# Two directions of a chunked recurrence in one level: a changed issue order on TensorE, and a side product made chunk by chunk

## The reference

```
def wkv_scan(state, r, w, a, b, k, v, reverse):
    def step(S, inp):
        r_t, w_t, a_t, b_t, k_t, v_t = inp
        sa = jnp.einsum('bhvk,bhk->bhv', S, a_t)
        S = S * w_t[:, :, None, :] + sa[..., None] * b_t[:, :, None, :] + v_t[..., None] * k_t[:, :, None, :]
        return S, jnp.einsum('bhvk,bhk->bhv', S, r_t)
    xs = tuple(jnp.moveaxis(t, 1, 0) for t in (r, w, a, b, k, v))
    state, y = lax.scan(step, state, xs, reverse=reverse)
```

```
    bonus = jnp.einsum('bthn,btdhn,hn->bth', rh, kh, r_k)[..., None] * v.reshape(B, T, RWKV_HEADS, RWKV_HEAD)
```

## Time and profile before

| | us |
|---|---|
| timed runs | 2593.86, 2598.66, 2600.04 (median 2598.66) |
| the profiled execution's own time | 2595.06 |
| its span | 2593.3 |
| PE busy | 2276.3 (88%) |
| DVE busy | 1158.6 (45%) |
| ACT busy | 727.4 (28%) |
| POOL busy | 390.9 (15%) |

### The profile page before, as it was taken

How to read it: one execution, slowest core, us unless ns; L and a number is a source line. 1 busy time by engine, 2 the same in 40 slices (tenths; PEclk the granted TensorE clock), 3 DMA queues, 4 the chain that set the end, 5 groups by cost and what they waited for, 6 DMA issues and landing times. The chain is left out here.

```text
span 2593.3 us, 47213 instructions
## 1 busy us (share of the span) xinstructions
PE 2276.3 (88%) x19058; PEld 1503.0 (58%) x19058; DVE 1158.6 (45%) x2561; ACT 727.4 (28%) x1698; POOL 390.9 (15%) x441
## 2 busy tenths in 40 slices
PE   6999989889979998899898679999888988888885
PEld 3444455548844444466565568877658876554453
DVE  3877765575542113632211563244576532531113
ACT  2010155465531002032222120024455531222220
POOL 0000000044340001122221000000034320222210
PEclk8999999999989999999999889999989999898997
DMA  9455401210016103699998642312310043899994
GB/s 379 195 213 237 166 33 43 81 43 5 4 50 259 73 0 118 253 385 397 371 355 316 271 173 98 129 67 94 103 39 5 4 157 125 348 414 384 380 376 170
DMA packets 80360, 474.27 MB, mean 183 GB/s; under 512 B 17296, under 2 KB 29200, under 8 KB 51728
## 3 DMA queue, kind: packets, MB, share of 16 engines
q1 hardware_dynamic: 55280, 419.82, 41.2%
q0 software_dynamic: 24864, 51.43, 5.2%
HBM read 439.99 MB, written 61.08 MB: 193 GB/s over the span
## 5 line engine op out<-in xcount | busy, mean ns | idle before, releaser
L2851 PE MATMUL xp_psG<-moe_ring,rt_xt 128*64 128x256 f32 (+1 forms) x2048 | 328.9, 406 | 39.7 <-DMA moe_ring<-in_moe 38.9
L2851 PEld LDWEIGHTS xp_psG<-moe_ring,rt_xt 128*64 128x64 f32 (+1 forms) x2048 | 228.5, 163 | 118.1 <-issue 56.8
L599 PE MATMUL win_ps<-h,win_ring 128*128 128x512 f32 x512 | 226.2, 600 | 5.4 <-PEq L292 5.4
L659 DVE SCALAR_TENSOR_TENSOR mod_acc<-ada_ring,cv_silu,mod_acc 128x512 f32<-128x512 f32 x280 | 198.0, 748 | 10.9 <-issue 0.4
L3108 DVE TENSOR_TENSOR rt_sg<-rt_sg,xp_psG 128x128 f32<-128x128 f32 x84 | 24.2, 288 | 335.9 <-ACT rt_sg L2925 335.9
L599 PEld LDWEIGHTS win_ps<-h,win_ring 128*128 128x128 f32 x512 | 97.0, 192 | 125.6 <-issue 125.6
L2872 PE MATMUL xp_psY<-moe_ring,rt_aT 128*64 128x512 f32 (+1 forms) x512 | 162.1, 602 | 2.9 <-DVE rt_aT L3115 2.9
L1274 POOL MEMSET ml_w<- 128x1536 f32 x4 | 5.4, 1376 | 765.3 <-POOLq L973 765.3
L2919 ACT ACTIVATE rt_xt<-xp_psT 128x512 f32<-128x512 f32 x168 | 90.9, 595 | 95.2 <-PE xp_psT L2836 89.4
L2178 PE MATMUL sc_ps<-sc_NT,sc_XI 64*64 64x64 f32 x2560 | 110.4, 225 | 8.2 <-issue 5.7
L2505 DVE TENSOR_TENSOR mg_gateb<-mg_gateb,mg_psY 128x512 f32<-128x512 f32 (+1 forms) x48 | 26.6, 554 | 192.1 <-PE mg_psY L2462 186.8
(11 more groups left out here) (539 smaller groups left out, 4302.0 us busy)
## 6 DMA issues: line engine op xcount, KB each, us to landing
moe_ring<-in_moe SPq DMA_DIRECT2D x128, 1536.0 KB, 16.1
ada_ring<-in_ada SPq DMA_DIRECT2D x22, 2048.0 KB, 14.8
win_ring<-in_win SPq DMA_DIRECT2D x20, 2048.0 KB, 8.2
cb_yg<-y_rows SPq DMA_DIRECT2D x16, 1024.0 KB, 13.1
mg_ring<-in_mg SPq DMA_DIRECT2D x16, 768.0 KB, 4.5
mg_wo<-in_wo SPq DMA_DIRECT2D x2, 4096.0 KB, 14.4
pr<-y_rows SPq DMA_DIRECT2D x8, 1024.0 KB, 17.7
ml_gate_ring<-in_mg SPq DMA_DIRECT2D x12, 512.0 KB, 3.6
```

Of the source, the lines that this page charges most:

```text
L599: last = pe.matmul(ps[:, n % NB, first(n):T], ring[:, j % 2, c, m * P:(m + 1) * P], h[:, c, first(n):T], start=c == 0, stop=c == KD - 1)
L659: last = dve.scalar_tensor_tensor(out=acc[:, a % 2, s], in0=aring[:, a % 3, c], scalar=weight, in1=acc[:, a % 2, s], op0=ALU.mult, op1=ALU ...
L2851: last = pe.matmul(psG[at:at + m, u % 2, 0:2 * P].rearrange("p (q n) -> p q n", q=2), xt[:, u % 2, c, at:at + m], ring[:, slot, c:2 * KD:K ...
```

## The change

1. The levels of both directions are issued together: `level(n, m)` waits for both directions, then issues d = 0 straight and d = 1 crossing, by turns. `place` lets direction 1 cross at every level, 0 and 5 too. The `across` waits are gone.
2. What `between` does is now put behind a level, for both directions: state products at m = 1, value products at m = 2, the transposes at m = 3, nothing at m = 4. The semaphore `onto` parts straight from crossing products in psR. The transposes are now products of 64x64 with the identity, in all four quarters; `first` parts the two groups of them.
3. ACT makes the right side at m = 2 between its two copies, and two strided copies of bk at m = 4 after each copy.
4. `state_and_rows` is split: state product and rows of the chunk before level 0, rows of the state behind it. `update` is split: `add_products` waits for the state product only, `decay` waits for the rows of the state.
5. `hat` has two buffers.
6. POOL makes the bonus per chunk of 64 tokens, all channels, between the operands of the steps; `queries` tells when a chunk's inputs are free.

The core of the diff:

```diff
-        hat = sb("hat", [P, KC, 2, L])
+        hat = [sb(f"hat{b}", [P, KC, 2, L]) for b in range(2)]
...
                 def step(n):
                     for m in range(1, 5):
                         for d in range(2):
                             copied(d, n, m)
-                            if n == 0 and m == d + 1:
+                            if n == 0 and m == 1:
                                 exponentials(d, 1)
-                            if m == 3:
-                                token_major(0, n, d)
+                            if m == 2:
+                                right_side(d, n)
                             if m == 4:
-                                token_major(*((0, n, 2), (1, n, 0))[d])
...
+                def bonus(j):
+
+                    f = j // NCH * NCH + max(j % NCH, NCH - 1 - j % NCH)
                     for d in range(2):
-                        operands(pool, d, n)
...
+                        w(pool, d, "queries", f)
+                    col = slice(j * L, (j + 1) * L)
+                    both, key = aa[:, 0, :, col], pr[:, K_T:K_T + KC, col]
...
+                ready = {3: (1,), 4: (2,), 5: (0,), 6: (3, 5), 7: (6, 4, 7)}
+                for n in range(1, NST):
+                    for d in range(2):
+                        operands(pool, d, n)
+                    for j in ready.get(n, ()):
+                        if j in outs:
+                            bonus(j)
...
-                def update(d, n):
-                    w(dve, d, "sy", n)
+                def add_products(d, n):
+
+                    w(dve, d, "s", n)
                     dve.tensor_tensor(S2[d][:], S[d][:], psS[d], ALU.add)
-                    dve.drain()
+
+                def decay(d, n):
+
+                    if n in outs:
+                        w(dve, d, "rows", n)
...
+                    def place(d, r, m):
+
+                        return HD - r if d and m % 2 else r
...
+                    for hp in range(KC):
+                        if m < 5:
+                            for d in range(2):
+                                for r in (0, HD):
+                                    to, wt, x = operands_of(d, hp, r)
+                                    pe.matmul(psW[d][to:to + HD, hp], wt, x, start=True, stop=True)
+                        for d in range(2):
+                            for r in (0, HD):
+                                to, wt, x = operands_of(d, hp, r)
+                                last = pe.matmul(psWT[d][to:to + HD, hp], x, wt, start=True, stop=True)
+                            if hp == KC - 1:
+                                last.then_inc(sem[d]["nn"].sem, 1)
...
                 def step(n):
                     for m in range(1, 6):
+                        level(n, m)
                         for d in range(2):
-                            level(d, n, m)
+                            between(d, n, m)
                     for d in range(2):
                         if n + 1 < NST:
                             matrices(d, n + 1)
                         corrections(d, n)
                     for d in range(2):
-                        state_and_rows(d, n)
-                        if n + 1 < NST:
-                            level(d, n + 1, 0)
+                        state_product(d, n)
+                        rows_of_chunk(d, n)
+                    if n + 1 < NST:
+                        level(n + 1, 0)
+                    for d in range(2):
+                        rows_of_state(d, n)
```

173 lines of the change are left out of this document (78 added, 95 removed).

## The result

The changed kernel takes 2627.03 us (median of 4, 2622.27 to 2636.52) against 2596.26 us of the kernel before in the same comparison: ratio 1.0124, 95% interval 1.0105 to 1.0142. It is slower by more than the noise, where 2580 us and faster were forecast.

The account below looks back on a forecast made before the run. PE was taken to set the pace inside a step, and POOL's bonus to bound the end of layer 0's stage. 2595.06 - 11.7 - 3.8 + 2.4 - 1.5 = 2580.5, so 2580 us, own range 2572 to 2590.

Parts of the forecast that it names:

- The tail: End of layer 0's recurrence stage: VectorE's 12.16 us idle behind POOL's bonus falls to 0.43, -11.7 us.
- The gaps and the unhindered step: Full recurrence step: waits of 1.10 to 1.77 us between levels; 10.5 + 9.3 = 19.8 us before unexplained idle time.
- The short steps of layer 1: Layer 1's first four steps, without output rows: 10.5 + 7.4 plus 0.3 = 18.2 us against 18.4, no gain.
- The unexplained idle time: PE idle without a releaser, 0.7 us per step; half was to vanish in the gaps, giving 20.1 us per full step.
- Rival 3: Recurrence steps: PE's idle time lowers the clock, a low-level step costs 14 us more, half the steps give 2690; 4%.
- clock 1.00 through the steps: Sign expected in the changed profile: PE's clock stays at its full level, 2.4 GHz, through the recurrence steps.
- Decay beside GpSimd: VectorE's decays before level 1, slowed by POOL's operands: bounded by 0 and 2 x 0.45 us, 0.3 per step taken.
- Exponentials in step 0: Behind level 1 of step 0, ACT makes four exponentials between its two copies: +1.2 us per layer, +2.4.
- Step 7: Last step of each layer: six pieces of 0.62 become four of 0.46, 0.15 and 0.93: -0.75 per layer, -1.5 us.
- Rival 1: PE throughput decides: fillers cover the evictions, a step loses 2.9 us, 46 in all, and the tail: 2537 us; 8%.
- rival 2: Recurrence slows by new waits (decay behind rows, ACT's queue, POOL beside DVE), +0.6 to +0.7 us per step: 2594; 14%.
- Rival 4: Layer 0's end: last bonus chunks wait for queries or POOL is slower beside DVE, the tail stays: 2592 us; 3%.

Follow-up runs that it names:

- the bonus alone: Kernel before with only the change's bonus part (two hat buffers, bonus sums chunk by chunk on GpSimd): 2579.0 us, ratio 0.9933.
- the small turns: Taken off: changed kernel with ACT copying both directions first, then hats turned by 8 products of 128x128 per step in place of 32 of 64x64: 2599.0 us, ratio 1.0012.
- the spare products: Changed kernel with four more 128x128 products per step that nobody reads, behind level 4 and ahead of level 1: 2621.52 us, ratio 1.0096.
- ACT's copies first: Changed kernel with ACT copying both directions in each level before exponentials, right sides and token-major copies: 2619.95 us, ratio 1.0098.
- the burst run: Kernel before with 1024 more 64x64 products of constants in layer 0 that wait for nothing and nobody reads: 2652.74 us, ratio 1.0208.
- the relieved kernel: Changed kernel with ACT's copies first and 128x128 turns: ratio 1.0012; with four unread products per step added: 2594.89 us, ratio 1.0000.
- the 16-bit run: Changed kernel with the factors and powers of levels 1 to 5 kept in 16 bits: 2574.16 us, ratio 0.9922.
- half the columns: Kernel before with level products, their evictions and masks on 32 of the 64 columns: 2598.26 us, ratio 1.0012.

## Why the prediction was wrong, step by step

- **The tail, -11.7 us.** Right: 12.16 became 0.44. The bonus alone gave -17.4 us (interval -23 to -12), and putting the old one back cost 18. So some 6 us beyond the tail hang on it in both orders; where they lie stays open.
- **The gaps and the unhindered step, 19.8 us.** Right in mechanism and half a microsecond short. The shortest intervals that the changed kernel showed in layer 0, from the matrices on, are 5.78 (to level 0), 3.54 (to level 1), 2.20, 2.48, 2.39, 2.50 (level to level) and 1.40 us (to the matrices), 20.3 in sum, 11.0 for the levels where the forecast had 10.5, and waits behind ACT and DVE are where they were named. Half a microsecond per step is more than the 0.3 of gain. The short steps of layer 1 were forecast at 17.9 and some idle time; their shortest intervals sum to 19.2. From the matrices to level 1 they take 8.3 us (5.31 and 3.03), where the forecast had 7.4, and the terms that it names for this add up to only 6.9. Even without a stall the changed order would have gained nothing: 9 full and 4 short steps take 259 us, and the same 13 with the bonus alone, stalls included, 260.
- **The unexplained idle time: the step that failed.** The forecast took 0.7 us per step from the earlier trace rows, could not say what it was, and "of which I let half vanish in the gaps": +0.35. It is PE waiting for its instructions. The changed order adds 112 instructions per step by the small turns (priced as time of PE alone, 0.47 twice, never as instructions) and puts what it has in bursts between gaps: stalls come in the very next levels. The six steps have a mean of 24.3 us, 4 above the unhindered one. With the clock held up by the spare products it was still 3.0 (23.3 us). With 7 packets fewer and ACT's copies first as well it was 20.9 us, 1.4 above that kernel's own shortest step of 19.5. An idle time without a releaser was treated as slack; it was the mark of the bound.
- **The clock.** Rival 3 had 4%, and what it described happened: "clock 1.00 through the steps" failed, and some 24 and 23 us went by at the low level. Its size was wrong, 14 us a step and 2690. Measured are 1.5 us at each matrices stretch at the low level and 20 us of excess in 13 steps, of which, with the clock held up, only 5 to 7 us came back, since waits for packets took their place.
- **Decay beside GpSimd, +0.3 us per step.** About right: median 0.61 in place of 0.43, twice a step, +0.36.
- **Exponentials in step 0, +1.2 per layer.** Levels 1 to 2 took 3.01 us there against 2.20, +0.8. **Step 7, -1.5**: could not be read out of steps that packets had lengthened.
- **Rival 1** (PE throughput) rested on four quarters at work giving their pace; the 4 times quoted there is a product of two factors of 2, an estimate. The pace is there in short bursts (64 records in 0.93 us), and the burst run shows that it can't be held: 3.81 us per 256 instructions at full clock, of which PE works 2.09.
- **Rivals 2 and 4.** The waits that rival 2 names are there, but alone they leave the full step at 20.3 us; its 2594 us was passed by the packets and the clock. Rival 4 did not come: the tail went.

The new order costs some 50 us against the bonus alone (ratios 1.0124 and 0.9933), 32 of them beyond the kernel before. In terms of runs, taken off one after the other: ACT's order 7 us, the small turns 21, the spare products in the relieved kernel 3, which is within the noise. What is left (1.0000 against 0.9933, 17 us) is the changed order with the same number of packets. In its trace 20 of the 26 us beyond the shortest intervals lie in intervals with a wait for a packet, against 1.4 at the low clock. No run takes these waits away and leaves the rest as it is, so that the bursts cause them is argued.

## What to carry to other kernels

In a stage of many small products count instructions as well as records: two per record, 256 to a packet of the instruction queue, and hold the count against the 3.8 us per packet of the burst (3.2 at the least, in the recurrences). Idle time of PE that nobody releases, inside a run of ready instructions and 1.3 to 1.5 us behind the landing of such a packet, is the mark of a bound. Then fewer instructions for the same work (one large transpose for four small products) are worth more than shorter waits: 21 us against 7 here. When a time falls after an edit, compare the shortest steps as well: the 16-bit run looked like a cure of the stalls, and it had shortened the work. Two costs that cover each other (packets and the clock) can't be priced by removing one; and independent parts of a change (here the bonus) should be priced, and tried, apart.

## What the runs showed of the hardware

- PE's instructions arrive in packets of 16 KB, 256 instructions each (7 packets more for 1792 instructions more, 16 for 4096), never less than 3.2 us apart in the recurrences of the two kernels and 3.8 us apart on average in a free burst at full clock, each 0.9 to 1.5 us long, while 256 instructions at hand run in 2.09 us.
- A product of 32-bit 64x64 operands leaves two load and two multiplication records, one of 16-bit operands one of each (x2560 against x1280), and a record takes 225 ns with 64 columns and 225 ns with 32 (means of the second half of a level, kernel before and half the columns).
- Time at the lower clock costs less than its length says where instructions are the bound: removing about 43 us of it gave 5 to 7 us, and the excess with waits for packets grew from 16.6 to 24.2 us.
- A VectorE multiply of two 128x256 float32 inputs takes 0.41 to 0.43 us with no GpSimd operation beside it, and up to 1.0 us beside one.
